# Attention scores one step ahead, and ten projection products spread over six of eight steps

## The reference, cut to what matters

```python
proj = h @ w_in                                   # q_lat (512), kv_lat (256), k_rope (32)
q  = (rms_norm(q_lat)  @ w_qb ).reshape(B, S, H, 96)     # 64 plain + 32 rotary columns per head
kv = (rms_norm(kv_lat) @ w_kvb).reshape(B, S, H, 128)    # 64 for k, 64 for v
s = where(causal, (q . k) * scale, MASK)          # per head, in blocks of 128 queries
p = softmax(s);  o = p @ v
```

## Time and profile before

| | |
|---|---|
| median of 3 runs | 3060.53 us (3057.98 to 3063.66) |
| profiled execution, span | 3070.7 us, with 40665 instructions |
| the changed loop in it | from 124.4 to 315.5 us |
| VectorE busy, whole span | 1724.5 us (56%) |
| ScalarE busy, whole span | 1245.4 us (41%) |

### The profile page before, as it was taken

The page is one execution under the profiler, slowest core; times in us unless marked ns, Lnnn a source line. Parts: engine busy times, 40 slices in busy tenths (PEclk is TensorE's granted clock), DMA queues, the critical chain, the costliest instruction groups (busy, mean ns, idle before and its releaser), DMA issues. The chain is left out here.

```text
span 3070.7 us, 40665 instructions
## 1 busy us (share of the span) xinstructions
PE 2858.4 (93%) x16535; PEld 2438.6 (79%) x16535; DVE 1724.5 (56%) x2989; ACT 1245.4 (41%) x2250; POOL 248.9 (8%) x224
## 2 busy tenths in 40 slices
PE   5988899999997989889999999899999998899998
PEld 4766787787886879789999997688788866678886
DVE  5666554435774866443468887543425386654344
ACT  3455432223433343323467776432223345432222
POOL 0000000000002452010000001112100002200000
PEclk7899999999999999889999999999999999999999
DMA  5222234422231111053479997211231203412321
GB/s 220 76 108 102 96 144 171 157 103 96 83 144 55 56 42 56 27 204 120 170 262 353 344 339 275 76 62 46 91 122 45 83 32 121 157 69 81 113 85 65
DMA packets 74418, 387.94 MB, mean 126 GB/s; under 512 B 8490, under 2 KB 10190, under 8 KB 42574
## 3 DMA queue, kind: packets, MB, share of 16 engines
q1 hardware_dynamic: 60816, 349.20, 31.2%
q10 hardware_dynamic: 10382, 26.07, 2.4%
q0 software_dynamic: 3024, 9.98, 0.9%
HBM read 368.43 MB, written 22.03 MB: 127 GB/s over the span
## 5 line engine op out<-in xcount | busy, mean ns | idle before, releaser
L342 DVE TENSOR_TENSOR wlo<-stage,whi 128x1024 fp32r<-128x1024 f32 (+4 forms) x524 | 533.7, 1059 | 350.8 <-ACT whi L354 350.1
L354 ACT ACTIVATE whi<-stage 128x1024 fp32r<-128x1024 f32 (+4 forms) x524 | 443.8, 896 | 211.2 <-PE ps L638 171.0
L638 PE MATMUL ps<-whi,mxhi 128*128 128x256 f32 x968 | 282.7, 292 | 13.3 <-DVE wlo L342 9.0
L638 PE MATMUL ps<-whi,mxlo 128*128 128x256 f32 x968 | 275.5, 285 | 0.0
L638 PE MATMUL ps<-wlo,mxhi 128*128 128x256 f32 x968 | 275.3, 284 | 0.0
L638 PE MATMUL ps<-bxhi,whi 128*128 128x512 f32 x480 | 200.9, 419 | 17.1 <-DVE bxlo L342 8.4
L638 PEld LDWEIGHTS ps<-whi,mxhi 128*128 128x128 f32 x968 | 186.7, 193 | 16.4 <-DVE wlo L342 6.2
L638 PE MATMUL ps<-bxhi,wlo 128*128 128x512 f32 x480 | 190.0, 396 | 0.0
L638 PE MATMUL ps<-bxlo,whi 128*128 128x512 f32 x480 | 189.7, 395 | 0.0
L638 PEld LDWEIGHTS ps<-wlo,mxhi 128*128 128x128 f32 x968 | 187.2, 193 | 0.0
L638 PEld LDWEIGHTS ps<-whi,mxlo 128*128 128x128 f32 x968 | 187.0, 193 | 0.0
(11 more groups left out here) (591 smaller groups left out, 6573.0 us busy)
## 6 DMA issues: line engine op xcount, KB each, us to landing
stage<-in_gu SPq DMA_DIRECT2D x91, 1024.0 KB, 6.7
more<-in_gu SPq DMA_DIRECT2D x41, 1024.0 KB, 6.7
stage<-in_ada SPq DMA_DIRECT2D x40, 1024.0 KB, 4.9
stage<-in_dn SPq DMA_DIRECT2D x36, 768.0 KB, 5.4
stage<-in_dn SPq DMA_DIRECT2D x32, 640.0 KB, 4.3
stage<-in_gin SPq DMA_DIRECT2D x16, 1024.0 KB, 4.8
stage<-in_gt SPq DMA_DIRECT2D x16, 1024.0 KB, 4.7
more<-in_dn SPq DMA_DIRECT2D x16, 640.0 KB, 4.6
```

Source lines behind the costliest of these rows:

```text
L342: return e.do.tensor_tensor(out, x, y, op)
L354: return e.do.activation(out, x, f, **kw)
L638: return self.p.do.matmul(out, lhsT, rhs, start=start, stop=stop, skip_group_check=True)
```

## The change

Scores are issued one step ahead: scores(0) before the loop, scores(n + 1) in step n. The order in a step is then scores(n+1), turn(n-3), values(n-4). The ten products go, two each, to the steps 0, 1, 3 and 4, and one each to 5 and 6. `queries` moves from step 3 to step 5 on both engines (on ScalarE it now stands ahead of the copy of the turned probabilities), `keys` from step 4 to step 6 behind that copy, and the split of the next wq from step 7 to step 6. The split of wk stays in step 2. For head pair 1 a call ahead of the loop replaces the one in step 2.

```diff
+        scores(0)
         for n in range(64 + 4):
-            if n % 8 == 0 and n < 56:
-                more = self.mla_project(L, n // 8 + 1)
-            step = more if n % 8 and n < 64 else iter(())
-            if n < 64:
-                scores(n)
-            next(step, None)
+            if n % 8 == 0:
+                more = self.mla_project(L, n // 8 + 1) if n < 56 else iter(())
+            if n < 63:
+                scores(n + 1)
+            if n % 8 in (0, 1, 3, 4, 6):
+                next(more, None)
             if 3 <= n < 67:
                 turn(n - 3)
-            next(step, None)
+            if n % 8 in (0, 1, 3, 4, 5):
+                next(more, None)
             if n > 3:
                 values(n - 4)
-            next(step, None)
...
         keys(0)
+        self.act_ahead("wq", 1, False)
...
             if n % 8 == 2 and g < 8:
-                self.act_ahead("wq", g, False)
                 self.act_ahead(f"wk{g}", 0, False)
-            if n % 8 == 4 and g < 8:
-                keys(g)
+            if n % 8 == 5 and g < 8:
+                queries(g)
...
-            if n % 8 == 3 and g < 8:
-                queries(g)
+            if n % 8 == 6 and g < 8:
+                keys(g)
...
-            if n % 8 == 7 and g < 7:
+            if n % 8 == 6 and g < 7:
                 self.act_ahead("wq", g + 1, False)
...
         self.dve_ahead("wk0", 0)
+        self.dve_ahead("wq", 1, False)
...
             if n % 8 == 2 and g < 8:
-                self.dve_ahead("wq", g, False)
                 self.dve_ahead(f"wk{g}", 0, False)
-            if n % 8 == 3 and g < 8:
+            if n % 8 == 5 and g < 8:
                 queries(g)
...
-            if n % 8 == 7 and g < 7:
+            if n % 8 == 6 and g < 7:
                 self.dve_ahead("wq", g + 1, False)
```

## The result

The changed kernel takes 3069.80 us (median of 10 runs) against 3063.74 us for the kernel before in the same sessions: ratio 1.0024, 95% interval 1.0015 to 1.0032. It is slower by 0.24%, some 7 us; forecast were +6.4 us. In the profiled executions the loop grew from 191.06 to 195.59 us, by 4.5.

What follows compares the result with a forecast made beforehand. The loop was taken as bound by TensorE with gaps, and by the clock. 183.6 us plus six clock losses of 2.3 gave 197.4 against 191.06; that +6.4 on 3060.5 gave 3067 us, range 3051 to 3081.

Steps and rivals of the forecast that it cites:

- What bounds the loop: In the loop before, TensorE's work with gaps of 0.3 to 1.9 us, and the clock, set the time.
- The bank rule and the chain of step 7: Values(3) waits for reduce(7), queued behind the wq split, 11.8 us after the query products; TensorE stands about 4.3 us.
- First values(3): First values of unit 3, in step 7, get their bank 21.6 us after scores(0).
- The period without the clock: One group, from values(3) of step 7 to the next: 11.8 + 13.3 = 25.1 us, without clock loss.
- TensorE's 13.3 us: TensorE's work from values(3) to the next end of the query products: 7.57, a modulation sum 0.42, eight products 5.36.
- The clock term: Low clock behind the stand in each of six groups: 2.3 us lost each, bounds 0 and 6.6.
- The rest, behind the last stand: Loop from the last values(3) of step 7 to its end, clock loss included: 38.8 us.
- The short waits: TensorE's waits for the queries copy in step 5, 0.65 us, and the keys copy in step 7, 0.9 us.
- The calls ahead of the loop: Calls for wq 1 before the loop issue nothing: 0 us; otherwise the split, 2.0, stands ahead of scores(0) once.
- the clock holds: Same stand in step 7, but no low clock behind it: loop 183.6 us, -7.5, time 3053; chance 0.13.
- The chain doesn't bind: No long stand in step 7: groups 20.8 us, loop 158, -33 us, time 3027; chance 0.10.
- Long low spells: Clock low for 11 to 13 us behind each stand, 5.9 lost a group: loop 219, +28 us, time 3088; chance 0.12.

Runs made afterwards that it cites:

- The fixed banks: The changed kernel with scores in banks 0 to 2 in turn, turns in bank 3 and values in bank 4; loop 197.0 us, ratio 1.0029.
- filling: The changed kernel with 16 unread matmuls between turn(4) and values(3) in step 7 of six groups; loop 179.7 us, ratio 0.9969.
- scores-ahead kernel: The kernel before with the scores issued one step ahead and nothing else; loop 216.4 us, ratio 1.0097.
- the fastest loop: The changed kernel with wq's low part in step 7 and, in step 5, the modulation piece ahead of the queries; loop 163.1 us, ratio 0.9915.

## Why the prediction was right

- *What bounds the loop*: right. TensorE's work, gaps, and the clock.
- *The bank rule and the chain of step 7*: right in place, releaser and price. Stands of 3.7 to 4.2 us, forecast 4.3; VectorE's wait before the low part 3.8, ScalarE's for the landing 0.44 (forecast 0.5 at most). First values(3) at 21.24 us, forecast 21.6. The fixed banks and both kernels with the low part in step 7 show each link by breaking it.
- *The period without the clock*, 25.1 us, was somewhat long: 27.13 less the 2.7 that filling gave back is 24.4. The landing took 3.7 us at the median, not 3.9, and TensorE's 13.3 us come out at some 13.0.
- *The clock term*, 2.3 us a group, was somewhat short: 2.7. The low stretches were 6.83 us in all six groups; I had weighed that length as one in three, and priced it at 3.4, as if TensorE worked through all of it; it works in 5.4 of the 6.83 us.
- These two errors cancel in part: forecast 27.4 a period, measured 27.1. The rest, behind the last stand, was forecast at 38.8 (with its clock loss) and is 38.7. The loop's +6.4 was +4.5. That the timed median came out at 3069.8 and its rise at 6 to 7 us, nearer to the forecast than the loop did, is luck in part: nothing in the sum gives those last 2 us.
- *The short waits*: in the group shown 0.51 for the queries copy, 0.55 for the keys copy, forecast 0.65 and 0.9. *The calls ahead of the loop* issued nothing, as said: the count of matmuls and of VectorE's instructions is unchanged.
- *The rivals*: "the clock holds" is what filling makes: 179.7, a gain of 11.4 against the 7.5 forecast. "The chain doesn't bind" came true only where the low part was moved. "Long low spells" didn't happen here, but in the scores-ahead kernel. That its loop is longer by 25.3 us, near the +28 given, proves nothing for the price: its spells are 17.1 us, not 11 to 13, and it has waits of its own.
- *Open*: the timed runs say 6 to 7 us and the loop 4.5; the two profiled spans differ by 1.2 only. Behind the loop the execution of the kernel before took 4.2 us more than the changed one, with 133 us at 1.2 GHz against 123. And its whole span, 3070.7, is at the slow end of that kernel's runs, 7 to 10 us above their medians. Since the clock falls in some of its groups only, its loop may be shorter in a usual execution than the 191.1 profiled, and the loss larger than 4.5. That would fit the remaining 2 us; with one profile of it, it isn't shown.

## What to carry to other kernels

When work is issued a step ahead in a rotation of buffers, ask anew which buffer each taker gets and whose release it waits for: here the values came to wait for the reduce of their own step, and any slow item queued ahead of that reduce became a stand. Place a wait where nothing is queued behind it: one line that put the low part behind the reduce was worth 31 us of loop. And price a wait of TensorE by what it does to the clock, not by its length alone: 10 and 16 us of this loop, before and after, were only that.

## What the runs showed of the hardware

- A wait of 1.44 us behind a step without products was enough, in all six groups of one kernel, to bring the clock to 1.2 GHz for 3.4 to 10.2 us. But the length of the wait alone doesn't tell: 1.68 us did so in one group of the kernel before and not in the next, waits of 0.94 us in that kernel with step 5 filled did not, and in the fastest loop the clock fell with no wait over 0.65 us just ahead.
- With scores, turns and values alone the clock didn't come back: in the kernel with only the scores ahead it was low for 17.1 us in every group, 8.65 us of them without a gap in TensorE's work, and came back 3.9 us after the products did. A clock that is up can stay up with such work: the last 17.3 us of the loop before ran at 1.00.
- Matmuls whose result nobody reads, put into a wait that exists anyway, paid: 96 of them made the loop 15.9 us shorter, 36 in another place 14.8. Put where there was no wait, 49 of them made the loop before 9.9 us longer.
- With the clock in play the parts of a change don't add up: +25.3 and +9.0 us singly, +4.5 together, -26.5 with one more line.
